# Turning the updated inverse in each doubling of a delta rule, in place of a matrix product

## The chip, the cores and the metric

The kernel runs on one core of a Trainium2 chip. The metric is the device time of one execution in microseconds (us). TensorE (PE) does matrix products and transposes into the eight banks of PSUM; VectorE (DVE) and ScalarE (ACT) work on SBUF and empty the banks; SyncE (SP) and GpSimd (POOL) issue transfers. Every engine works through its own instructions in a fixed order and waits on semaphores.

## The reference

Two layers in a row on 512 tokens of width 1024, in float32: a first block (spatial gating, differential attention, a mixture of 32 experts), then a second with a gated delta rule and stick-breaking attention. The change lies in the delta rule: four heads of width 128, in chunks of 64 tokens. For each chunk and head it needs the solution of a unit lower triangular system, then walks over the chunks:

```python
m = jnp.where(strict, beta[..., :, None] * kk * decay, 0.0)
sol = lax.linalg.triangular_solve(eye + m, rhs, left_side=True, lower=True, unit_diagonal=True)
...
def step(state, inp):
    v_new = u_c - jnp.einsum('bhck,bhkv->bhcv', w_c, state)
    o = (jnp.einsum('bhck,bhkv->bhcv', qd_c, state) + jnp.einsum('bhij,bhjv->bhiv', qk_c, v_new))
    state = state * ge_c[..., None, None] + jnp.einsum('bhck,bhcv->bhkv', kd_c, v_new)
```

## The kernel before

The delta rule works on four tiles of 128 tokens (two chunks each); all operations of a tile take the four heads together, as one 128x512 piece. The inverse of `eye + m` is built by doubling. The tensor `TT` holds the transposed inverse of the diagonal blocks of the present size, and `TI` the inverse, which is the same matrix turned. Level 0 sets blocks of two (`TT` = identity minus the masked matrix, line 1941), and `TI` is got by turning `TT` (line 1053, copied out of PSUM by ScalarE, line 2617). Each level l from 1 to 5 (`LEVELS` is 6) then takes the off-diagonal part `BT` of that level (VectorE masks it, lines 1944 and 1952), forms `Q` = BT^T TI on TensorE (line 1058), which ScalarE copies to SBUF (line 2623), and then Q^T TT (line 1062), which VectorE subtracts from `TT` (line 1965). Levels 1 to 4 form TT^T Q right behind it (line 1064), which VectorE subtracts from `TI` (line 1963), ahead of the subtraction from `TT`. Level 5 needs no new `TI`. After the levels come the products `nw` and `u` (lines 1068 and 1070), and then, tile after tile and for both chunks c of a tile, the state: `wS` (line 1076), VectorE's `vn` (line 1979), the products `kv` and `qS` (lines 1080 to 1094, whose instructions have lines 1084, 1091 and 1092), and VectorE's update of the state `S` (lines 1985 and 1988), from which the next `wS` starts. Beside the state steps of tiles 0 and 1, tiles 2 and 3 are prepared: `turn_keys`, `decays` and `turn_weighted` on TensorE, `weigh`, `weigh_turned` and `differences` on VectorE.

The order is written by generators that every engine runs in the same way. `delta_tile` yields between its pieces; it has 17 pieces: 0 (`kk`, `qk`, `qdT`), 1 (the first `TI`), 2 to 11 (two for each level), 12 (`nw` and `u`), 13 to 16 (the state). `chain(0)` runs tiles 0 and 2, `chain(1)` tiles 1 and 3; a chain waits at "state" until the tile before it is finished. A round takes one piece of each chain, and after each of the two one step of a third generator, `beside_steps`: on TensorE a step is three f32r matmuls of 128x512 (lines 543 to 545) of the projection `qb` (32 steps), then 2 * PAUSE = 10 empty steps, then `kb` (32 steps), then 10 empty ones. On VectorE and ScalarE the steps of `beside_steps` hold the splits of the next weights into two parts (ScalarE's `whi`, VectorE's `wlo`), the squares and copies of finished blocks, and after each projection its norm: sums, an inverse root, and one 128x2048 product (line 2022), which all fall into steps 33 and 34 for `qb` and 75 and 76 for `kb`; another split falls into step 38. When the chains have ended, the steps left run on without a pause.

PSUM banks are handed out by the class `Banks`: `take` gives the bank that was filled longest ago, and the first matmul into it waits until what it held before has been copied out; a projection block holds its bank until its last matmul. After the chains, TensorE turns `qb` (16 transposes, line 1225) and starts the projection `vb` (lines 1226 to 1232 and 1235 to 1238), whose four blocks are tied by hand to banks 4 to 7, and whose first step waits for what bank 4 held before:

```python
turn_block("qb", 0, beside_nat["qb"], ve["qb", 0, "normed"])
for c in range(HB):
    bank.take(("vb", 0, c), BANKS - HB + c)
value_columns(0, 0)
value_columns(0, 1)
value_columns(0, 2)
turn_block("kb", 0, beside_nat["kb"], ve["kb", 0, "normed"])
value_columns(0, 3)
claim(0, 2)
stick_scores(0)
```

Beside this ScalarE squares the whole output of the delta rule (line 2700), copies the turned `qb` (2701), makes a split, takes the root `dout` (2703) and copies the turned `kb` (2704). VectorE makes its split, builds small constants, sums the squares (line 2059), scales the output (2065, four instructions) and clears two banks (2109), for which the first scores (line 1180) of the stick-breaking attention wait.

Of the kernel before, what the change touches and what calls it, by code (L numbers as in the profile page):

```python
# [109 lines left out]
def build(nc, x, norm1_g, w_in, v_norm_g, w_s, b_s, q_norm_g, k_norm_g, lambda_q1, lambda_k1,  # L110
# [418 lines left out]
    def tensor(e):  # L529
# [509 lines left out]
        def delta_tile(i):  # L1039
            kT_, kbT, _, qdT, _, dec, MT, TI, TT, qkT, nwT, GR = sets[i % 2]  # L1040
            qT_, kd = qT_of[i], kd_of[i]
            BT, Q = kT_, kbT
            Kn, Qn, Vn = (heads(NAT[:, i, n * NH:(n + 1) * NH]) for n in (1, 0, 2))
            on.wait_ge(*ac["out", "kT", i])
            on.wait_ge(*ac["out", "kbT", i])
            mm4(i, "kk", kT_, kbT)
            on.wait_ge(*ac["out", "qT", i])
            mm4(i, "qk", kT_, qT_)
            on.wait_ge(*ve["qd", i])
            turn4(i, "qdT", Qn)  # L1050
            yield
            on.wait_ge(*ve["TT", i, 0])
            turn4(i, "TI", TT)
            yield
            for l in range(1, LEVELS):
                on.wait_ge(*ve["BT", i, l])
                on.wait_ge(*(ac["out", "TI", i] if l == 1 else ve["out", ("TI", l - 1), i]))
                mm4(i, ("Q", l), BT, TI)
                yield
                on.wait_ge(*ac["out", ("Q", l), i])  # L1060
                on.wait_ge(*ve["TT", i, l - 1])
                mm4(i, ("TT", l), Q, TT)
                if l < LEVELS - 1:
                    mm4(i, ("TI", l), TT, Q)
                yield
            on.wait_ge(*ve["rk", i])
            on.wait_ge(*ve["TT", i, LEVELS - 1])
            mm4(i, "nw", Kn, TT)
            on.wait_ge(*ve["bv", i])
            mm4(i, "u", TT, Vn)  # L1070
            yield "state"
            for c in range(2):
                R = slice(64 * c, 64 * c + 64)
                on.wait_ge(*ac["out", "nw", i])
                on.wait_ge(*(ve["state", i, c - 1] if c else ve["state", i - 1, 1] if i else ve["state0"]))
                mm4(i, ("wS", c), nwT, S)
                if i < 2:
                    (turn_weighted if c else turn_keys)(i + 2)
                yield
                ps = heads(fresh(("kv", c), i))  # L1080
                on.wait_ge(*ve["kd", i])
                on.wait_ge(*ve["out", ("wS", c), i])
                for h in range(DH):
                    m = e.matmul(ps[:, h, :], kd[R, h, :], vn[R, h, :], start=True, stop=True)
                m.then_inc(*pe.mark(("kv", c), i))
                bank.filled((("kv", c), i))
                ps = heads(fresh(("qS", c), i))
                on.wait_ge(*ac["out", "qdT", i])
                on.wait_ge(*ve["qkT", i])
                for h in range(DH):  # L1090
                    e.matmul(ps[:, h, :], qdT[:, h, :], S[:, h, :], start=True, stop=False)
                    m = e.matmul(ps[:, h, :], qkT[R, h, :], vn[R, h, :], start=False, stop=True)
                m.then_inc(*pe.mark(("qS", c), i))
                bank.filled((("qS", c), i))
                if i < 2 and c == 0:
                    decays(i + 2)
                yield
# [178 lines left out]
    def vector(e):  # L1276
# [5 lines left out]
        def settle():  # L1282

            on.wait_ge(*ve.now())
# [645 lines left out]
        def delta_tile(i):  # L1930
            kT_, kbT, _, qdT, _, dec, MT, TI, TT, qkT, nwT, GR = sets[i % 2]
            BT, Q, u_, kd = kT_, kbT, qT_of[i], kd_of[i]
            Kn, Qn, Vn = (heads(NAT[:, i, n * NH:(n + 1) * NH]) for n in (1, 0, 2))
            on.wait_ge(*pe["kk", i])
            on.wait_ge(*ac["decay", i])
            tt(MT, heads(inside("kk", i)), dec, MUL).then_inc(*ve.mark("out", "kk", i))
            on.wait_ge(*pe["qk", i])
            settle()
            tt(BT, MT, each(level[0]), MUL).then_inc(*ve.mark())
            settle()  # L1940
            tt(TT, each(ident), BT, SUB).then_inc(*ve.mark("TT", i, 0))
            yield
            settle()
            tt(BT, MT, each(level[1]), MUL).then_inc(*ve.mark("BT", i, 1))
            tt(qkT, heads(inside("qk", i)), dec, MUL).then_inc(*ve.mark("out", "qk", i))
            settle()
            tt(qkT, qkT, each(causal), MUL).then_inc(*ve.mark("qkT", i))
            yield
            for l in range(1, LEVELS):
                if l < LEVELS - 1:  # L1950
                    on.wait_ge(*pe[("Q", l), i])
                    tt(BT, MT, each(level[l + 1]), MUL).then_inc(*ve.mark("BT", i, l + 1))
                if l == 2:
                    on.wait_ge(*pe["kbT", i])
                    tt(Kn, Kn, spread(egc, i), MUL).then_inc(*ve.mark("rk", i))
                if l == 3:
                    tt(Vn, Vn, spread(betaf, i), MUL).then_inc(*ve.mark("bv", i))
                yield
                on.wait_ge(*pe[("TT", l), i])
                if l < LEVELS - 1:  # L1960
                    on.wait_ge(*pe[("TI", l), i])
                    settle()
                    tt(TI, TI, heads(inside(("TI", l), i)), SUB).then_inc(*ve.mark("out", ("TI", l), i))
                settle()
                tt(TT, TT, heads(inside(("TT", l), i)), SUB).then_inc(*ve.mark("TT", i, l))
                ve.also("out", ("TT", l), i)
                yield
            on.wait_ge(*pe["u", i])
            e.tensor_copy(u_, heads(inside("u", i))).then_inc(*ve.mark("out", "u", i))
            yield "state"  # L1970
            for c in range(2):
                R = slice(64 * c, 64 * c + 64)
                on.wait_ge(*pe[("wS", c), i])
                if c:
                    on.wait_ge(*pe[("qS", 0), i])
                elif i:
                    on.wait_ge(*pe[("qS", 1), i - 1])
                settle()
                tt(vn[R], u_[R], heads(inside(("wS", c), i))[R], ADD).then_inc(*ve.mark("out", ("wS", c), i))
                if i < 2:  # L1980
                    (differences if c else weigh)(i + 2)
                yield
                on.wait_ge(*pe[("qS", c), i])
                settle()
                tt(S, S, spread(gend[:, c * N16:(c + 1) * N16], i), MUL).then_inc(*ve.mark())
                settle()
                on.wait_ge(*pe[("kv", c), i])
                tt(S, S, heads(inside(("kv", c), i)), ADD).then_inc(*ve.mark("state", i, c))
                ve.also("out", ("kv", c), i)
                if i < 2 and c == 0:  # L1990
                    weigh_turned(i + 2)
                yield
# [176 lines left out]
    def scalar(e):  # L2169
# [440 lines left out]
        def delta_tile(i):  # L2610
            kT_, kbT, _, qdT, _, dec, MT, TI, TT, qkT, nwT, GR = sets[i % 2]
            Q = kbT
            Vn = heads(NAT[:, i, 2 * NH:3 * NH])
            on.wait_ge(*(ve["tiles clear"] if i < 2 else ve["finished", i - 2]))
            turn4(i, "qdT", qdT)
            yield
            turn4(i, "TI", TI)
            yield
            for l in range(1, LEVELS):
                on.wait_ge(*pe[("Q", l), i])  # L2620
                if l > 1:
                    on.wait_ge(*pe[("TI", l - 1), i])
                act(Q, heads(inside(("Q", l), i)), ACT.Copy).then_inc(*ac.mark("out", ("Q", l), i))
                yield
                yield
            on.wait_ge(*pe["nw", i])
            act(nwT, heads(inside("nw", i)), ACT.Copy, scale=-1.0).then_inc(*ac.mark("out", "nw", i))
            yield "state"
            for c in range(2):
                R = slice(64 * c, 64 * c + 64)  # L2630
                if i < 2 and c:
                    turn_weighted(i + 2)
                    weighted(i + 2)
                elif i < 2:
                    turn_keys(i + 2)
                yield
                on.wait_ge(*pe[("qS", c), i])
                act(Vn[R], heads(inside(("qS", c), i))[R], ACT.Copy).then_inc(*ac.mark("out", ("qS", c), i))
                yield
# [386 lines left out]
```

## Time and profile before

| | us |
|---|---|
| median of 3 runs | 1445.6 (1444.33 to 1446.9) |
| the profiled execution, its own time | 1444.63 |
| its span, first to last instruction | 1442.9 |
| TensorE busy | 1324.2 (92%) |
| VectorE busy | 660.4 (46%) |
| ScalarE busy | 495.6 (34%) |
| delta rule with what runs beside it | about 989 to 1160 of the span |

A start time in the rows counts from the first instruction of the span. Busy TensorE is not TensorE at its peak, since matmuls overlap; the pitch from one start to the next says what a matmul costs in a stream. A float32 product of 128x128 shows as two matmul records, so a product for four heads is "x8"; a turn of four heads is "x4". "PS" is PSUM. Line 1019 is any product of four heads, line 540 any transpose, line 2188 any ScalarE operation, line 1295 VectorE's part of a split.

### The profile page before, as it was taken

The numbers are of one execution on the slowest core, as the hardware profiler recorded it, in microseconds if no ns is written. First come the engines' busy times: TensorE is split into PE (matmuls) and PEld (weight loads), VectorE is DVE, ScalarE is ACT, GpSimd is POOL, SyncE is SP. The second block draws the span as 40 slices with busy tenths as digits, with TensorE's granted clock in tenths as the row PEclk, the third lists the DMA queues.
The fourth block names the chain that finished last, engine by engine and source line by source line (L and its number), as shares of the span: only waits on it lengthen the run. The fifth ranks groups of instructions, "written<-read, shape, count | busy, mean of one in ns | idle before, by whom it ended". The sixth has DMA issues, their size and how long they took to land.

```text
span 1442.9 us, 16794 instructions
## 1 busy us (share of the span) xinstructions
PE 1324.2 (92%) x7035; PEld 1018.0 (71%) x7035; DVE 660.4 (46%) x1091; ACT 495.6 (34%) x770; POOL 59.3 (4%) x70
## 2 busy tenths in 40 slices
PE   6999999999999996788887889989989988899998
PEld 5888887678766885545554468777968875488887
DVE  4454334655466446211111178657566455413253
ACT  4334234556355423011111155354232145422231
POOL 0000000000000000111111100000000001000000
PEclk9999999999999997699999999999999999899999
DMA  6222322112222368899999952102010020112331
GB/s 223 88 86 88 117 67 80 59 59 88 88 88 88 121 244 325 342 402 401 409 401 409 371 193 88 59 1 88 2 57 1 30 88 6 54 59 89 116 117 59
DMA packets 67558, 207.41 MB, mean 144 GB/s; under 512 B 9003, under 2 KB 10141, under 8 KB 55190
## 3 DMA queue, kind: packets, MB, share of 16 engines
q1 hardware_dynamic: 61234, 192.11, 35.5%
q0 software_dynamic: 5536, 12.04, 2.8%
q10 hardware_dynamic: 708, 2.13, 0.4%
q8 instruction: 57, 0.93, 0.3%
q14 instruction: 23, 0.19, 0.0%
HBM read 196.33 MB, written 17.83 MB: 148 GB/s over the span
## 4 chain that ended last, share of the span: by engine, by line
PE 71%; DVE 9%; DMA 8%; ACT 6%; issue 3%; SPq 1%; POOL 1%; ACTq 0%; POOLq 0%; DVEq 0%
PE PS L543 17%; PE PS L545 16%; PE PS L544 16%; PE PS L1019 5%; DMA work<-xn_scratch,slot_tokens 4%; PE PS L540 4%; PE PS L862 3%; DMA raw<-in_w 2%; DVE wlo L1295 2%; PE PS L890 2%; ACT work L2188 1%; SPq L2888 1%; ACT whi L2188 1%; ACT scratch L2188 1%; PE PS L707 1%
## 5 line engine op out<-in xcount | busy, mean ns | idle before, releaser
L1295 DVE TENSOR_TENSOR wlo<-raw,whi 128x2048 fp32r<-128x2048 f32 x72 | 164.9, 2291 | 277.6 <-ACT whi L2188 277.5
L2188 ACT ACTIVATE whi<-raw 128x2048 fp32r<-128x2048 f32 x72 | 137.6, 1911 | 235.3 <-PE PS L545 218.6
L543 PE MATMUL PS<-whi,hthi 128*128 128x512 f32 x480 | 195.6, 407 | 6.2 <-ACT y_plain L2188 4.1
L543 PE MATMUL PS<-hthi,whi 128*128 128x512 f32 x480 | 196.7, 410 | 0.9 <-DVE htlo L1328 0.9
L545 PE MATMUL PS<-whi,htlo 128*128 128x512 f32 x480 | 188.2, 392 | 0.0
L545 PE MATMUL PS<-hthi,wlo 128*128 128x512 f32 x480 | 187.7, 391 | 0.0
L544 PE MATMUL PS<-wlo,hthi 128*128 128x512 f32 x480 | 187.6, 391 | 0.0
L544 PE MATMUL PS<-htlo,whi 128*128 128x512 f32 x480 | 187.4, 390 | 0.0
L2188 ACT ACTIVATE work<-PS 128x512 f32<-128x512 f32 (+3 forms) x148 | 81.4, 562 | 301.0 <-PE PS L862 71.7
L543 PEld LDWEIGHTS PS<-hthi,whi 128*128 128x128 f32 x480 | 90.5, 188 | 32.5 <-issue 14.2
L543 PEld LDWEIGHTS PS<-whi,hthi 128*128 128x128 f32 x480 | 90.8, 189 | 24.5 <-ACT y_plain L2188 4.3
L545 PEld LDWEIGHTS PS<-whi,htlo 128*128 128x128 f32 x480 | 90.4, 188 | 19.4
L545 PEld LDWEIGHTS PS<-hthi,wlo 128*128 128x128 f32 x480 | 90.2, 188 | 19.4
L544 PEld LDWEIGHTS PS<-wlo,hthi 128*128 128x128 f32 x480 | 90.9, 189 | 16.0 <-issue 0.2
L544 PEld LDWEIGHTS PS<-htlo,whi 128*128 128x128 f32 x480 | 90.5, 189 | 15.7 <-issue 0.2
L540 PEld LDWEIGHTS PS<-consts,work 128*128 128x128 f32 x456 | 59.8, 171 | 48.3 <-DMA work<-xn_scratch,slot_tokens 23.7
L540 PE MATMUL PS<-consts,work 128*128 128x128 f32 x456 | 70.8, 301 | 24.8 <-DMA work<-xn_scratch,slot_tokens 15.6
L2188 ACT ACTIVATE scratch<-PS 128x512 f32<-128x512 f32 (+3 forms) x80 | 41.8, 533 | 107.8 <-PE PS L540 53.1
L543 PE MATMUL PS<-yhi,whi 128*128 128x512 f32 x192 | 75.7, 394 | 0.3 <-DVE wlo L1295 0.3
L545 PE MATMUL PS<-yhi,wlo 128*128 128x512 f32 x192 | 74.8, 389 | 0.0
L544 PE MATMUL PS<-ylo,whi 128*128 128x512 f32 x192 | 74.8, 389 | 0.0
L862 PE MATMUL PS<-y_plain,work 128*64 128x256 f32 x208 | 40.5, 417 | 4.8 <-ACT work L2188 2.5
(356 smaller groups left out, 1839.2 us busy)
## 6 DMA issues: line engine op xcount, KB each, us to landing
raw<-in_w_in SPq DMA_DIRECT2D x44, 1024.0 KB, 5.0
y_plain<-in_w SPq DMA_DIRECT2D x21, 1024.0 KB, 26.1
w_plain<-in_w SPq DMA_DIRECT2D x20, 1024.0 KB, 22.7
h_plain<-in_w SPq DMA_DIRECT2D x20, 1024.0 KB, 25.7
raw<-in_w SPq DMA_DIRECT2D x15, 1024.0 KB, 20.6
merged<-in_w SPq DMA_DIRECT2D x10, 1024.0 KB, 28.0
scratch<-in_w SPq DMA_DIRECT2D x10, 1024.0 KB, 30.1
raw<-in_w_gate SPq DMA_DIRECT2D x8, 1024.0 KB, 5.1
```

What stands on the lines that cost most here:

```text
L540: return e.transpose(o, i, ident[0:n, 0:n])
L543: e.matmul(o, lh, rh, start=start, stop=False)
L544: e.matmul(o, lh, rl, start=False, stop=False)
L545: return e.matmul(o, ll, rh, start=False, stop=stop)
L707: e.matmul(ps[:, 0:w], qT[64 * c:64 * c + 64, h, i * P:i * P + P], kT[64 * c:64 * c + 64, h, 0:w], start=True, stop=True).then_inc(*pe.mar ...
L862: t = e.matmul(ps[rows_, 0:DE], TOK[:, u, k, rows_], w[x][:, k, :], start=k == 0, stop=k == KD - 1)
L890: t = e.matmul(ps[rows_, :], HT[:, u, k, rows_], w[x][:, k, cols], start=k == 0, stop=k == 1)
L1019: m = e.matmul(ps[:, h, :], l[:, h, :], r[:, h, :], start=True, stop=True)
L1295: tt(lo, raw_place(j), as_f32(hi), SUB).then_inc(*ve.mark("lo", j))
L2188: return e.activation(o, i, f, bias=bias, scale=scale)
L2888: e.dma_start(place(raw_place(j)), src).then_inc(*raw_got[raw_slot[j]].mark(j))
```

## The change

The transposed inverse `TT` is updated first, in every level as before, and levels 1 to 4 then turn the new `TT` on TensorE and let ScalarE copy the result over `TI`. The product TT^T Q and VectorE's subtraction from `TI` are gone. A level l of 1 to 4 now has three pieces in place of two, and a tile 21 in place of 17. `beside_steps` is as it was.

```diff
@@ tensor, delta_tile
             for l in range(1, LEVELS):
                 on.wait_ge(*ve["BT", i, l])
-                on.wait_ge(*(ac["out", "TI", i] if l == 1 else ve["out", ("TI", l - 1), i]))
+                on.wait_ge(*(ac["out", "TI", i] if l == 1 else ac["out", ("TI", l - 1), i]))
                 mm4(i, ("Q", l), BT, TI)
                 yield
                 on.wait_ge(*ac["out", ("Q", l), i])
                 on.wait_ge(*ve["TT", i, l - 1])
                 mm4(i, ("TT", l), Q, TT)
+                yield
                 if l < LEVELS - 1:
-                    mm4(i, ("TI", l), TT, Q)
-                yield
+                    on.wait_ge(*ve["TT", i, l])
+                    turn4(i, ("TI", l), TT)
+                    yield
@@ vector, delta_tile
                 yield
                 on.wait_ge(*pe[("TT", l), i])
-                if l < LEVELS - 1:
-                    on.wait_ge(*pe[("TI", l), i])
-                    settle()
-                    tt(TI, TI, heads(inside(("TI", l), i)), SUB).then_inc(*ve.mark("out", ("TI", l), i))
                 settle()
                 tt(TT, TT, heads(inside(("TT", l), i)), SUB).then_inc(*ve.mark("TT", i, l))
                 ve.also("out", ("TT", l), i)
                 yield
+                if l < LEVELS - 1:
+                    yield
@@ scalar, delta_tile
                 if l > 1:
-                    on.wait_ge(*pe[("TI", l - 1), i])
+                    on.wait_ge(*pe[("TT", l - 1), i])
                 act(Q, heads(inside(("Q", l), i)), ACT.Copy).then_inc(*ac.mark("out", ("Q", l), i))
                 yield
                 yield
+                if l < LEVELS - 1:
+                    turn4(i, ("TI", l), TI)
+                    yield
```

## Rows read from the trace of the kernel before

**Rows 1.** Stretches of the span: busy us of each engine, granted clock, DMA.

```profile
1020.00:1040.00 20.00, 20.00 (x147) 18.61 (x146) 9.46 (x14) 4.95 (x8) 0.00 (x0) 1.00 0.00 1
...
1060.00:1080.00 20.00, 14.46 (x94) 12.53 (x93) 16.31 (x24) 5.89 (x10) 0.00 (x0) 0.91 0.13 40
```

**Rows 2.** The chain that ended last, one level of tiles 0 and 1.

```profile
1001.79 1.78 PE PS L1019 x16
...
1006.75 0.89 PE PS L1019 x8
1008.34 0.89 PE PS L1019 x8
1009.92 1.78 PE PS L1019 x16
```

**Rows 3.** The same chain: decays, a turn of four heads, and a state step.

```profile
1050.08 1.05 PE PS L1031 x2
...
1095.25 0.44 PE PS L540 x4
...
1145.91 0.69 DVE scratch L1979
1146.65 1.16 PE PS L1084 x8
...
1151.17 0.70 DVE scratch L1985
1151.90 0.70 DVE scratch L1988
1152.64 1.17 PE PS L1019 x8
```

**Rows 4.** VectorE and ScalarE in time: split, subtractions and a copy in level 1.

```profile
1001.98 2.29 DVE L1295 TENSOR_TENSOR wlo<-raw,whi 128x2048 fp32r<-128x2048 f32 x1 [1.45 <-ACT whi L2188]
...
1005.00 0.69 DVE L1963 TENSOR_TENSOR y_plain<-y_plain,PS 128x512 f32<-128x512 f32 x1
...
1007.68 0.60 ACT L2188 ACTIVATE y_plain<-PS 128x512 f32<-128x512 f32 x1 [5.25 <-PE PS L1019]
```

**Rows 5.** VectorE and TensorE in time: norm of `qb` and TensorE's wait.

```profile
1061.02 0.68 DVE L1287 TENSOR_REDUCE smalls<-y_plain 128x8 f32<-128x512 f32 x1
...
1063.14 2.29 DVE L2022 TENSOR_TENSOR raw<-raw,smalls 128x2048 f32<-128x2048 f32 x1
...
1067.61 1.11 PE L540 MATMUL PS<-consts,y_plain 128*128 128x128 f32 x4 [5.54 <-DVE y_plain L1941]
```

**Rows 6.** TensorE in time, from the last state step to the first scores.

```profile
1159.01 0.50 PE L543 MATMUL PS<-whi,hthi 128*128 128x512 f32 x1
...
1165.78 0.50 PE L543 MATMUL PS<-whi,hthi 128*128 128x512 f32 x1 [4.08 <-ACT y_plain L2188]
...
1180.24 0.93 PE L1180 MATMUL PS<-y_plain 64*128 64x128 f32 x8
```

**Rows 7.** ScalarE and VectorE in time behind the chains.

```profile
1162.09 1.91 ACT L2188 ACTIVATE scratch<-work 128x2048 f32<-128x2048 f32 x1
...
1174.92 2.50 DVE L2065 TENSOR_TENSOR work<-work,smalls 128x512 f32<-128x512 f32 x4
1177.80 0.70 DVE L2109 MEMSET PS<- 128x768 f32 x1 [0.38 <-ACT y_plain L2188]
```

**Rows 8.** TensorE in time: the instruction behind a wait, at two places.

```profile
632.37 1.16 PE L540 MATMUL PS<-consts,work 128*128 128x128 f32 x8 [2.69 <-DMA work<-xn_scratch,slot_tokens]
...
733.47 1.16 PE L540 MATMUL PS<-consts,work 128*128 128x128 f32 x8 [2.35 <-DMA work<-xn_scratch,slot_tokens]
```

**Rows 9.** Stretches, TensorE alone: busy us, granted clock, DMA share, GB/s.

```profile
634.00:637.00 3.00, 2.64 (x14) 0.50 1.02 382
...
733.00:736.00 3.00, 1.70 (x14) 1.00 1.02 429
...
1167.00:1169.00 2.00, 2.00 (x7) 0.50 0.00 0
```

## Prediction

> **What bounds the kernel now.** I read the stretches of the span first. In the doubling levels of tiles 0 and 1 TensorE is busy for all of 20 us while VectorE works for 9.5 and ScalarE for 5; in the 20 us around the state of those tiles TensorE stands still for 5.5 [rows 1]. DMA is nearly idle in both, so SP's queue decides nothing here, and POOL has no work. The chain that ended last says the same of the levels: products of line 1019 with the projection's f32r steps between them, and no other engine [rows 2]. So in the levels TensorE's work is the time; in the state steps, and where no projection step stands between two pieces, the hops to VectorE and back are. The change touches both, so I go through the stage round by round.
>
> **Prices.** A four-head product costs 0.89 us and, with the projection step behind it, 1.59, so the step costs 0.70 [rows 2]. A turn of four heads costs 0.44 [rows 3]. `kv` with `qS` runs from 1146.65 to just before VectorE's 1151.17, 4.4 us; `decays` 1.05 [rows 3]. VectorE's 128x512 operation takes 0.69 and about 0.1 passes before it starts, ScalarE's copy 0.60, a split 2.29 on VectorE [rows 4]. From the end of `qS` through the two updates of `S` to the next `wS` pass 1.55 us; from the end of a `wS` through `vn` to `kv` about 0.9 [rows 3].
>
> **The edits one by one.** Sixteen products TT^T Q go and sixteen turns come (four levels, four tiles): 16 x (0.89 - 0.44) = 7.2 us less on TensorE. VectorE loses sixteen subtractions, 16 x 0.69 = 11 us, ScalarE gains sixteen copies, 16 x 0.60 = 9.6. Neither moves the time of the levels by itself: it is busy half or a quarter of it [rows 1]. The new dependence is longer: product, subtraction, turn, copy, next product. With a projection step behind each piece the turn stands 0.70 + 0.89 + 0.70 = 2.3 us behind its product and needs 0.1 + 0.69; the next `Q` stands 0.70 + 0.44 + 0.70 = 1.8 behind the turn and needs 0.1 + 0.60. Covered. Without those steps the cover is gone, and here lies the cost: the sixteen extra pieces are extra rounds, and the 64 projection steps are handed out two to a round. No DMA or queue is moved.
>
> Before, tile 0 has 17 pieces, tile 2 starts in round 17, tile 1 takes up its state in round 18, tile 3 starts in round 22, and all ends in round 38; steps 1 to 32 fill rounds 0 to 15, 43 to 74 fill 21 to 38, so the last one sits behind the last state step, at 1159.01 [rows 6]. After, with 21 pieces, tile 2 starts in round 21, tile 3 in 26, and the last state step is in round 46. The projection steps stay in rounds 0 to 15 and 21 to 36. Rounds 16 to 20 are now the state of tile 0, and rounds 37 to 46 have none at all.
>
> *Rounds 2 to 15.* A pair of levels costs 2 x 1.59 + 2 x 1.59 + 2 x 1.14 = 8.62 us and carries six projection steps; before it costs 8.13, from 1001.79 to 1009.92 [rows 2], with four. One stall comes: in level 1 the split ends at 1004.27 on VectorE and the mask of tile 1 follows, so the first subtraction from `TT` can only run at 1005.00, where that from `TI` ran [rows 4]. TensorE reaches the turn at 1004.97 and goes on at 1005.8: 0.8 us. Level 1's first product started at 998.6, so level 5 ends at 998.6 + 4 x 8.62 + 6.34 + 0.8 = 1040.25.
>
> *Rounds 16 to 20, bare.* From 1040.25: four products of `nw` and `u` (3.6), `wS` and two turns (to 5.3). VectorE has two copies of `u`, a sum, the inverse root and the 2.29 us product of the norm, whose last sum to its start takes 1.44 behind the 0.68 [rows 5]; it is free at 7.3, `vn` ends at 8.0: TensorE waits 2.8. `kv`, `qS` and `decays` to 13.7; a wait of 0.6 for `S`; `wS` and the turned keys to 15.7. VectorE's order is now `S`, two weighings, the split of step 38, then `vn`, which ends at 18.7: a wait of 3.0. Tile 2's first piece follows, and its first turn starts at 27.1, at 1067.35. Before, the same norm stood ahead of tile 2's first operations, and this turn started at 1067.61 after a wait of 5.54 [rows 5]. So half of the levels' saving is already gone: I am 0.3 us and two projection steps (1.4 us) ahead, for 3.6 us of work saved.
>
> *Rounds 21 to 36.* Every piece is covered. Adding the pieces of rounds 22 to 36 (tile 1's state 13.0, tile 2 to level 5, tile 3 to level 3, 30 projection steps) gives 54.5 us, with some 0.3 of refilling: 1122.1.
>
> *Rounds 37 to 46, bare.* Here `nw` and `u` of tile 2 with the norm of `kb` on VectorE, whose 2.29 us stand ahead of `vn`; then tile 2's state against tile 3's level 4 and 5; then tile 3's `nw`, `u` and state alone. Work 29.8 us; waits 1.1 (ScalarE's copy of `Q` behind the root), 2.2 (`vn` behind the norm), 1.15 (`S`), 1.45 (`TT` behind `S`), 0.85, 1.6 and 0.85 in the last state steps, sum 9.2. The last `qS` ends at 1122.1 + 39.0 = 1161.1, against 1159.0 before [rows 6]: **2.1 us later**.
>
> *Behind the chains* comes something back. Before, TensorE turned `qb` and then waited 4.08 us until 1165.78 for a ScalarE copy [rows 6]: written out, bank 4 held the third turned `qb` block, and ScalarE came to these copies late, behind the norm of `kb` and the 1.9 us square [rows 7]. Writing out the takes of the new order, the turned blocks land in banks 0, 6, 3, 1 and bank 4 holds the last `qS`, copied out 0.7 us after its end. So `vb` starts at once. ScalarE's square starts at 1.55 behind the last `qS` and not at 3.08, since the norm of `kb` is long done, and all that hangs on it moves by 1.5. VectorE's scaling of the output started at 15.9 behind that end, took 2.5 [rows 7], and will start at 14.4; the clearing of two banks ends at 17.65. TensorE has 14.4 us of work until then. The first scores start at 17.7 instead of 1180.24 - 1159.0 = 21.2 [rows 6]: **3.5 us sooner**, with a new wait of 3.2 us. Behind them everything keeps its distances.
>
> Sum so far: 2.1 - 3.5 = -1.4 us.
>
> **The clock.** Behind a wait of 2.69 us the granted clock fell to 0.50, that is 1.2 GHz, and behind one of 2.35 it stayed at 1.00 [rows 8, 9]; it was 0.50 behind the wait of 4.08 as well [rows 9]. Such a fall costs about 1.6 us: the stretch after 1165.78 that ran at half speed lasted some 3.4 us. The old prices above contain two falls, at both long waits. The new order has three waits of about 3 us (2.8, 3.0, 3.2), all above 2.69, but my sums for them are good to 0.5 only. None falling gives -1.4, each adds 1.6, three give +3.4. I take two: +1.8.
>
> A turn's price is also where a page speaks against the change. The trace has 0.44 us for four transposes of 128x128 in float32, 0.11 each [rows 3]. The Trainium skill (TensorE: Matmul & The Clock Gate, Part 4: PE-mode transpose) gives about 275 ns for a 128x128 transpose in one kernel's context. Taken as a pitch, that would be an estimate of 16 x 4 x 0.275 = 17.6 us for the new turns against the 14.2 of the removed products: TensorE would have 3.4 us more to do and not 7.2 less, and the sum would be 10.6 us higher, near 1458. The trace differs from it and decides, so this gets no chance of its own; a page's 275 ns may be the length of one transpose that the next overlaps.
>
> **Rivals.** (1) *Slower:* all three waits let the clock fall, or the norm's and the split's place in front of `vn` costs more than 2.8 and 3.0. It decides from waits above 2.69 us on; price +3.4, 1449.0. For it: all three sums lie above that. Against: each hangs on a chain of eight terms. Part of this family is that `vb` still waits for ScalarE; then the sum is 2.1 - 1.5 + 1.6 x 2, also near +3.4. (2) *Faster:* TensorE's work bounds the stage throughout and the 7.2 us stay, 1438.4. For it: 20 of 20 us busy [rows 1]. Against: 5.5 us of waiting in the state steps, and ten more rounds without cover. (3) *Faster by a little more than can be seen:* no fall of the clock and waits shorter than mine, -3 or so, 1442.5. (4) That the change does not do what it says: both ways give the same `TI`, and the counts of instructions follow from the code; no chance worth a number.
>
> **The numbers.** The profiled execution took 1444.63 with a span of 1442.9, 1 us under the median of 1445.6; the difference of +1.8 is put on the median: 1447.4. A measurement of this kernel tells about 0.2% (2.9 us) from no change. Chances: forecast with zero to two falls 0.55, rival (1) 0.31, rivals (2) and (3) 0.14. Range: to -3.4 below, for rival (3), and to +4.9 above, for rival (1) with one wait mis-sized by 1.5: 1442.2 to 1450.5; rival (2) is left out. Faster 0.14, same 0.55, slower 0.31.
>
> **What would show it.** TT^T Q gone, and turns (x4) in its place; 21 pieces per tile; TensorE busy without a break in the levels of tiles 0 and 1 but for 0.8 us in the first; waits near 3 us ahead of both `kv` of tile 0, the first on the norm, the second on the split; no projection step behind about 1122; waits of 0.9 to 2.2 until about 1161; `vb` right behind the turned `qb`; the first scores waiting on VectorE's clearing. I am wrong if waits of more than 1 us show between 1070 and 1120, if the last `qS` ends before 1158 or after 1166, or if `vb` waits again.

## The result, and the profile after

| | before | after |
|---|---|---|
| median of the runs, us | 1446.13 (4 runs) | 1458.05 (4 runs) |
| ratio, 95% interval | | 1.0087 (1.0074 to 1.0100) |
| profiled execution: time, span | 1444.63, 1442.9 | 1455.09, 1453.3 |
| first product of the stage to the first scores | 989.39 to 1180.24, 190.9 | 989.26 to 1193.04, 203.8 |

The change makes the kernel 12 us (0.87%) slower. The forecast was 1447.4, in a range from 1442.2 to 1450.5; the measured time lies 7.5 us above that range. The profiled execution after is the fastest of its four runs, 3 us under the median. In it the stage from the first `kk` to the first scores is 12.9 us longer; some 2.4 us come back behind the stage, up to the end of the span, most of it because one stretch at the lower clock lasted 3.4 us there and 6.8 before. Every ratio here and below is taken against runs of the kernel before from the same session (medians 1446.13, then 1445.75 for e1 to e4 and 1444.76 for e5 to e7), with one slow run of the kernel before (1537.51) and one of e2_spread (3683.58) left out.

The instructions changed as the code says. The page of the changed kernel, its first part:

```profile
span 1453.3 us, 16660 instructions
PE 1331.7 (92%) x6971; PEld 1022.7 (70%) x6971; DVE 649.6 (45%) x1075; ACT 505.2 (35%) x786; POOL 59.3 (4%) x70
```

TensorE has 64 matmul records less than before: 128 of the products (eight for each of sixteen) went, 64 transposes came. VectorE has 16 operations and 10.8 us less, ScalarE 16 and 9.6 us more. But TensorE's busy time rose by 7.5 us (1324.2 before), where 7.2 less were due.

Stretches of the changed kernel's span; they answer to [rows 1], and the column before the last two is the granted clock:

```profile
1020.00:1040.00 20.00, 20.00 (x137) 18.01 (x136) 8.82 (x11) 7.69 (x11) 0.00 (x0) 1.00 0.16 53
1040.00:1060.00 20.00, 16.36 (x86) 13.11 (x85) 10.99 (x17) 7.17 (x11) 0.00 (x0) 0.75 0.00 1
1060.00:1080.00 20.00, 18.66 (x102) 15.40 (x100) 10.95 (x16) 4.70 (x8) 0.00 (x0) 0.82 0.17 53
1120.00:1140.00 20.00, 17.04 (x108) 14.96 (x106) 10.23 (x16) 5.38 (x12) 0.00 (x0) 0.89 0.17 54
1140.00:1160.00 20.00, 17.56 (x92) 14.46 (x92) 5.51 (x8) 2.98 (x5) 0.00 (x0) 0.77 0.00 1
1160.00:1180.00 20.00, 17.71 (x72) 13.95 (x71) 3.45 (x5) 4.52 (x6) 0.00 (x0) 0.66 0.00 1
```

The clock column can be read as a price: 20 us at a mean of 0.75 have lost 20 x 0.25 = 5.0 us of full speed. The five stretches below 1.00 give 5.0 + 3.6 + 2.2 + 4.6 + 6.8 = 22.2 us. Before, two stretches of this stage stood below 1.00, both at 0.91: 3.6 us. This price is an upper bound, since part of the slow time passes in waits and, as shown below, not all work takes twice as long at half the clock. The rounds that carry projection steps ran at 1.00 in both kernels. All runs agree with this: the mean clock of the whole execution was 0.955 to 0.959 in the four runs after, and 0.965 to 0.972 in the runs of the kernel before.

The waits of TensorE in time, at which the bare rounds can be followed (the bracket at the end of a line is the wait ahead of it, and what ended it):

```profile
1005.48 0.66 PE L540 MATMUL PS<-consts,y_plain 128*128 128x128 f32 x4 [0.76 <-DVE y_plain L1963]
1049.09 1.17 PE L1086 MATMUL PS<-scratch,y_plain 64*128 64x128 f32 x8 [3.63 <-DVE scratch L1979]
1061.88 1.16 PE L1086 MATMUL PS<-scratch,y_plain 64*128 64x128 f32 x8 [1.34 <-DVE scratch L1979]
1132.00 1.16 PE L1019 MATMUL PS<-scratch 128*128 128x128 f32 x8 [0.81 <-ACT scratch L2188]
1135.31 1.98 PE L1086 MATMUL PS<-scratch,y_plain 64*128 64x128 f32 x8 [2.14 <-DVE scratch L1979]
1144.58 2.08 PE L1019 MATMUL PS<-scratch,y_plain 128*128 128x128 f32 x8 [0.46 <-DVE scratch L1988]
1155.44 1.16 PE L1019 MATMUL PS<-scratch,work 128*128 128x128 f32 x8 [1.21 <-DVE scratch L1963]
1159.22 1.16 PE L1086 MATMUL PS<-scratch 64*128 64x128 f32 x8 [0.77 <-DVE scratch L1979]
1165.21 1.25 PE L1019 MATMUL PS<-scratch,work 128*128 128x128 f32 x8 [1.51 <-DVE scratch L1988]
1167.24 2.07 PE L1086 MATMUL PS<-scratch 64*128 64x128 f32 x8 [0.78 <-DVE scratch L1979]
1193.04 0.93 PE L1182 MATMUL PS<-y_plain 64*128 64x128 f32 x8 [1.07 <-DVE PS L2109]
```

These are the waits of the forecast, each where it was put and on the engine that was named, but for one of 0.6 for `S`, which did not come: together 14.5 us, against 19.6 forecast. There is none in front of `vb`: the bank walk was right as well (the 4.08 us of [rows 6] are gone).

TensorE alone in stretches of 2 us, around the waits of 3.63, 1.34, 2.14 and 1.51 (busy us, granted clock, DMA):

```profile
1046.00:1048.00 2.00, 0.00 (x0) 1.00 0.00 0
1048.00:1050.00 2.00, 0.91 (x8) 1.00 0.00 0
1050.00:1052.00 2.00, 2.00 (x8) 0.53 0.00 0
...
1060.00:1062.00 2.00, 0.66 (x4) 0.91 0.00 0
1062.00:1064.00 2.00, 2.00 (x13) 0.94 0.90 233
1064.00:1066.00 2.00, 2.00 (x7) 0.50 0.75 291
...
1068.00:1070.00 2.00, 2.00 (x9) 0.50 0.00 0
1070.00:1072.00 2.00, 2.00 (x16) 0.85 0.00 0
...
1134.00:1136.00 2.00, 0.69 (x3) 0.86 0.00 0
1136.00:1138.00 2.00, 2.00 (x10) 0.50 0.01 4
...
1148.00:1150.00 2.00, 2.00 (x12) 0.73 0.00 0
...
1164.00:1166.00 2.00, 0.79 (x7) 1.00 0.00 0
1166.00:1168.00 2.00, 1.22 (x7) 0.54 0.00 0
...
1178.00:1180.00 2.00, 2.00 (x8) 0.55 0.00 0
```

Here is what the forecast lacked. Behind the wait of 3.63 the clock was 0.50 for 10.2 us, with work on TensorE all the time, and behind a wait of only 1.34 it fell again, for 6.8 us. Towards the end of the stage it was 0.50 from about 1135.4 to 1149.1 behind the wait of 2.14, and from 1166.2 to 1179.8 behind the wait of 1.51, 13.7 us each (the wait of 0.78 came when the clock was already down). TensorE's timeline shows the cost on the pieces:

```profile
1050.19 0.80 PE L1093 MATMUL PS<-scratch,y_plain 128*128 128x128 f32 x2
1050.91 0.79 PE L1094 MATMUL PS<-scratch,y_plain 64*128 64x128 f32 x2
...
1160.30 0.49 PE L1093 MATMUL PS<-scratch 128*128 128x128 f32 x2
1160.72 0.48 PE L1094 MATMUL PS<-scratch,work 64*128 64x128 f32 x2
```

At 1.00 a pair of records of `qS` has a pitch of 0.42, at 0.50 of 0.72: half the clock makes this work 1.7 times as long, and not twice.

### The profile page after: what moved, and what is told of

It reads as the page before. It is cut to its first block, busy times and chain, and to the rows that moved or that the text cites. A ratio compares the mean times of both kernels' runs of the same rounds, so it can differ in the third digit from the quotient of the medians.

```text
span 1453.3 us, 16660 instructions
## 1 busy us (share of the span) xinstructions
PE 1331.7 (92%) x6971; PEld 1022.7 (70%) x6971; DVE 649.6 (45%) x1075; ACT 505.2 (35%) x786; POOL 59.3 (4%) x70
## 4 chain that ended last, share of the span: by engine, by line
PE 70%; DVE 10%; DMA 9%; ACT 5%; issue 3%; SPq 2%; POOL 1%; POOLq 0%; ACTq 0%; DVEq 0%
PE PS L543 17%; PE PS L545 16%; PE PS L544 16%; DMA work<-xn_scratch,slot_tokens 5%; PE PS L540 4%; PE PS L1019 4%; PE PS L862 3%; DMA w_plain<-in_w 2%; DVE wlo L1297 2%; SPq L2891 2%; ACT work L2188 1%; PE PS L1094 1%; PE PS L1093 1%; ACT whi L2188 1%; PE PS L707 1%
## 5 line engine op out<-in xcount | busy, mean ns | idle before, releaser
L543 PEld LDWEIGHTS PS<-hthi,whi 128*128 128x128 f32 x480 | 90.8, 189 | 32.5 <-issue 14.5
L545 PEld LDWEIGHTS PS<-hthi,wlo 128*128 128x128 f32 x480 | 90.4, 188 | 19.6
L2188 ACT ACTIVATE scratch<-PS 128x512 f32<-128x512 f32 (+3 forms) x88 | 46.7, 539 | 96.7 <-PE PS L540 60.6
```

Source lines behind the costliest of these rows:

```text
L543: e.matmul(o, lh, rh, start=start, stop=False)
L545: return e.matmul(o, ll, rh, start=False, stop=stop)
L2188: return e.activation(o, i, f, bias=bias, scale=scale)
```

## Experiments

Theory A: the loss is the slow clock in rounds in which TensorE has no projection step, whatever the two edited operations are. Theory B: the turn, its copy and the longer chain of dependences cost it. Theory C: the waits alone cost it.

**e1_rounds**, the rounds of the change without the change: products kept, an empty third piece (the same two lines on all three engines).

```diff
                     mm4(i, ("TI", l), TT, Q)
                 yield
+                if l < LEVELS - 1:
+                    yield
```

> The kernel before with an empty third piece in levels 1 to 4: the rounds of the changed kernel, but the products TT^T Q kept and nothing turned. Theory A (the loss is TensorE's slow clock in rounds without a projection step; turns and products play no part): the clock falls in the same places as after the change (granted clock near 0.5 for stretches of 5 to 13 us), and the time is that of the changed kernel plus the 7.2 us of work that the turns save, about 1465. Theory B (the loss comes from the turn, its copy and the longer chain of dependences): about the time before, 1446, at most 1450.

Measured: 1464.23, ratio 1.0128 (1.0101 to 1.0155). This is theory A's number (1465), 6 us above the changed kernel; a kernel with no turn of `TI` beyond level 0 loses more than the changed one. Its stretches below 1.00, TensorE alone:

```profile
1040.00:1060.00 20.00, 16.37 (x91) 0.82 0.10 40
1060.00:1080.00 20.00, 18.73 (x99) 0.76 0.16 53
...
1140.00:1160.00 20.00, 17.05 (x72) 0.71 0.00 0
1160.00:1180.00 20.00, 16.54 (x68) 0.59 0.00 1
1180.00:1200.00 20.00, 20.00 (x89) 0.77 0.21 71
```

That is 3.6 + 4.8 + 5.8 + 8.2 + 4.6 = 27 us of full speed, in the same rounds and just behind them. The extra pieces alone bring the loss, so theory B is out as its cause.

**e2_spread**, the change with the projection steps held back in eight rounds (the same lines on all three engines):

```diff
+    BARE = (4, 7, 10, 13, 28, 31, 34, 37)
...
+        round_ = 0
         while chains:
             for c in list(chains):
                 if next(c, "end") == "end":
                     chains.remove(c)
-                next(beside, None)
+                if round_ not in BARE:
+                    next(beside, None)
+            round_ += 1
```

> The changed kernel, but rounds 4, 7, 10, 13, 28, 31, 34 and 37 hand out no projection step on any engine, so that the 64 steps reach to the last state step as before the change. Each of the eight rounds then waits some 0.3 us for the copy of the turned TI. Theory A: the clock falls only where it fell before; 7.2 us of work saved less about 3 of waits: about 1442, faster than before. Theory B: the turns and copies are all still there, so about 1458.

Measured: 1441.81, ratio 0.9979 (0.9969 to 0.9989): faster than before, as theory A said (1442). The same turns, copies and dependences as in the changed kernel, 16 us less. In the stage its clock stood below 1.00 only at the two long waits that the kernel before has too, 0.83 in both stretches where that had 0.91. In the profiled execution this takes most of the stage's gain back: 190.2 us from the first `kk` to the first scores, 0.7 less than before; the other 2.3 of the 3.0 us by which its span is shorter lie outside the stage. The waits for the copy were fewer than forecast, and the two longest were 0.79 and not 0.3:

```profile
1015.58 1.16 PE L1020 MATMUL PS<-y_plain,work 128*128 128x128 f32 x8 [0.79 <-ACT y_plain L2195]
1023.86 1.16 PE L1020 MATMUL PS<-y_plain,work 128*128 128x128 f32 x8 [0.79 <-ACT y_plain L2195]
```

**e3_joined**, the turn in one piece with the next `Q`, a projection step between (TensorE's part, as it reads against the kernel before):

```diff
             for l in range(1, LEVELS):
+                if l > 1:
+                    on.wait_ge(*ve["TT", i, l - 1])
+                    turn4(i, ("TI", l - 1), TT)
+                    next(beside, None)
                 on.wait_ge(*ve["BT", i, l])
                 ...
                 mm4(i, ("Q", l), BT, TI)
-                yield
+                yield "taken" if l > 1 else None
                 ...
                 mm4(i, ("TT", l), Q, TT)
-                if l < LEVELS - 1:
-                    mm4(i, ("TI", l), TT, Q)
                 yield
```

(ScalarE's copy of the turned `TI` stands ahead of its wait for `Q`, and the main loop leaves out its own projection step after "taken".)

> The turn of TI stands in the same piece as the next Q, with one projection step between the two on TensorE, so a tile keeps 17 pieces and all projection steps stay in their old rounds. A pair of levels costs 7.24 us and not 8.13. Theory A: 7.2 us less than before less a few short waits for copies (about 0.1 each): 1439 to 1441. Theory B: the chain of dependences is the same as after the change, so it loses again: 1450 or more.

Measured: 1449.95, ratio 1.0028 (1.0018 to 1.0038). A miss: 10 us above what I had put under theory A. Its trace says why:

```profile
1088.24 1.16 PE L1019 MATMUL PS<-y_plain,work 128*128 128x128 f32 x8 [1.78 <-ACT y_plain L2188]
1120.51 1.16 PE L1019 MATMUL PS<-y_plain,work 128*128 128x128 f32 x8 [1.02 <-ACT y_plain L2188]
```
```profile
1088.00:1090.00 2.00, 1.76 (x14) 1.00 0.00 0
1090.00:1092.00 2.00, 2.00 (x10) 0.59 0.00 0
...
1100.00:1102.00 2.00, 2.00 (x15) 0.85 0.00 0
```

One projection step (0.70) does not cover the hop turn, copy, `Q`: two `Q` start 0.53 late, and two wait 1.78 and 1.02 for ScalarE. Behind the 1.78, in front of tile 1's state products, the clock fell to half for 10.2 us, another 5 us of full speed. This is not a round without projection steps; one stood right in front of the wait and the next behind the state products, at 1096.21. So theory A named the right cost, but a covered round is not safe from it. That a wait this short can stand in front of a fall is the same thing that the forecast missed, and I missed it twice.

**e4_filled**, the changed kernel with twelve useless products in the waits of the bare rounds (those without projection steps):

```diff
+        FILL = {("kv", 0, 0): 3, ("kv", 1, 0): 1, ("kv", 0, 2): 2, ("kv", 0, 3): 1, ("kv", 1, 3): 1,
+                ("wS", 1, 0): 1, ("wS", 1, 2): 1, ("wS", 1, 3): 1, ("nw", 0, 3): 1}
+
+        def filler(ps, *key):
+            for _ in range(FILL.get(key, 0)):
+                e.matmul(ps, ident, C[:, 4 * P:8 * P], start=True, stop=True)
...
```

(`filler` is called right behind `fresh`, ahead of the waits of each `nw`, `wS` and `kv`; the first number of a key is the chunk, the second the tile.)

> The changed kernel with twelve float32 products of 128x512 over constants (1.05 us each at full clock, their result is written over) put into the waits in front of kv, wS and nw of the rounds without a projection step. The work that counts is unchanged and nothing is sooner for VectorE or ScalarE. Theory A: the clock stays at 1.00 in these rounds or falls for less, and the time drops by 8 to 15 us below the changed kernel, to 1443 to 1450. If the waits themselves were the loss (theory C: my waits were undersized), the filler changes nothing or adds a few us: 1458 to 1463.

Measured: 1448.53, ratio to before 1.0022 (1.0011 to 1.0033): some 9.5 us below the changed kernel, with 12 products more. TensorE alone:

```profile
1040.00:1060.00 20.00, 17.22 (x101) 0.99 0.05 6
1060.00:1080.00 20.00, 20.00 (x100) 0.75 0.13 48
...
1140.00:1160.00 20.00, 19.20 (x112) 1.00 0.00 0
1160.00:1180.00 20.00, 19.41 (x105) 1.00 0.20 67
```

The clock stays up in the last state steps. It falls for 10.2 us behind a wait of 1.73 (5.0 us of full speed), and once more, for 3.4 us, at the end of a wait of 3.37 in front of the first scores. The filler makes nothing else start sooner, so what it gains comes through the clock: theory C is out as well, and at least these 9.5 us of the changed kernel's time are the clock's.

**e5_products_spread**: e1_rounds with the rounds of e2_spread left empty (both diffs above). It prices the swap alone.

> The products TT^T Q kept, 21 pieces a tile, the eight empty rounds of e2_spread: e2_spread without its turns. Theory A (only the slow clock in rounds without a projection step lost time, and a turn is worth 7.2 us over a product on TensorE): the order is nearly that before the change, so 1446, some 4 us above e2_spread, which gave back part of the 7.2 in waits for copies and a longer slow stretch. Theory B (turn and copy cost as much as they save): no more than 1442, the time of e2_spread.

Measured: 1446.19, ratio 1.0007 (0.9999 to 1.0016). As theory A said. Against it e2_spread is 4.4 us lower by medians from two sessions, 4.0 by their ratios: that is what turns are worth in these rounds. A little over half of the 7.2 us of TensorE's work became time. Waits for copies of 1.8 us in e2_spread's trace (0.79, 0.79 and 0.25) are part of the rest, which was not traced in full.

**e6_even**: the changed kernel, single steps held back in place of whole rounds, so that every hop has one projection step.

```diff
+    BARE = [(r, 0) for r in (4, 7, 10, 13)] + [(r, 1) for r in (5, 8, 11, 14)] + [(r, 0) for r in range(28, 36)]
...
-            for c in list(chains):
+            for n, c in enumerate(list(chains)):
...
-                next(beside, None)
+                if (round_, n) not in BARE:
+                    next(beside, None)
```

> The changed kernel with sixteen single projection steps left out of its rounds, in place of eight whole rounds, so that one step stands between any two pieces that depend on each other (the last step again falls behind the last state step). Theory A: the waits of 0.79 us for copies in e2_spread go, and a fall of the clock stays only at the two long waits that the kernel before has: 1439 to 1441, below e2_spread's 1441.8. If the time saved does not depend on where the steps stand: 1442 as e2_spread.

Measured: 1439.7, ratio 0.9966 (0.9954 to 0.9978): 5 us faster than before, the best of all. The waits for copies are gone from the levels, as expected. In its trace the wait in front of `vb` is short as well, and the clock stays up there, which I had not expected:

```profile
1160.00:1180.00 20.00, 16.33 (x87) 1.00 0.45 157
1163.16 0.50 PE L544 MATMUL PS<-whi,hthi 128*128 128x512 f32 x1 [0.75 <-ACT y_plain L2195]
1176.30 0.93 PE L1186 MATMUL PS<-y_plain 64*128 64x128 f32 x8 [2.92 <-DVE PS L2116]
```

Its stage took 1176.30 - 991.64 = 184.7 us (the start is that of its first `kk`), 6.2 less than before. The wait in front of `vb` is 3.3 us shorter than before and the one in front of the scores 2.9 longer, and no fall of the clock follows there, so part of these 6.2 us may come from there and not from the levels; this was not separated.

**e7_before_filled**: the kernel before, with four such products in its wait of 5.54 us.

```diff
+            ps = fresh("TI", i)
+            for _ in range(4 if i == 2 else 0):
+                e.matmul(ps, ident, C[:, 4 * P:8 * P], start=True, stop=True)
             on.wait_ge(*ve["TT", i, 0])
-            turn4(i, "TI", TT)
+            for h in range(DH):
+                m = turn(heads(ps)[:, h, :], TT[:, h, :])
...
```

> The kernel before with four float32 products of 128x512 over constants (4.2 us, written over by the turn) in the wait of 5.54 us in front of the first turn of tile 2; nothing else. Theory A: the clock no longer falls there; that stretch at half clock lasted 2.8 us and more in other runs, so 1.4 to 3 us less than before: 1443 to 1444.5. If the fall's price is hidden by VectorE's work behind it: no difference.

Measured: 1445.11, ratio 1.0002 (0.9993 to 1.0011): no difference, where 1.4 to 3 us were expected. The clock did stay at 1.00 in the stretch from 1060 to 1080, and in the profiled execution the way from the first `kk` to the first product of `vb` is 1.5 us shorter than before: 174.9 us (992.10 to 1166.98) for 176.4 (989.39 to 1165.78). But the wait of 4.08 in front of `vb` is still there, and behind it the lower clock now lasted 6.8 us and not 3.4:

```profile
1166.98 0.80 PE L543 MATMUL PS<-whi,hthi 128*128 128x512 f32 x1 [4.08 <-ACT y_plain L2194]
1160.00:1180.00 20.00, 15.93 (x76) 0.83 0.30 106
```

Up to the first scores 0.7 us of the gain is left. All runs together say the same: the mean clock of the whole execution is 0.969 in the eleven runs of this kernel and 0.969 in the 23 of the kernel before. So the filler removed a fall that cost about what I had priced it at, in its place, and won no clock on the whole. Why the next one lasted longer is not shown.

## Why the prediction was wrong, point by point

- **Work taken off TensorE**: right. Turns for products are worth 7.2 us of its work; by medians, e2_spread against e5 shows 4 us of it as time where the projection steps are spread, and e6_even against the kernel before 5 us. That the measured 1458 is also the sum which the prediction worked out for transposes of 275 ns is luck: four turns of `TI` take 0.36 us here (0.09 each) from their start to the next instruction's at full clock, and e1_rounds, without these turns, took 6 us longer still.
- **Rounds and cover**: right. 21 pieces leave rounds 16 to 20 and 37 to 46 without projection steps, and TensorE waits there where the forecast has it. Of the single sizes the wait on the norm was larger (3.63 for 2.8), those on the split and on `S` smaller (1.34 for 3.0; 0.46 for 1.15), both behind work at half clock, with which TensorE arrives later; the one at the scores was 1.07 for 3.2, likewise.
- **Behind the chains**: right. `vb` starts without a wait, and the first scores came 18.0 us behind the last `qS` (1175.0 to 1193.04), 17.7 forecast, 21.2 before. But this last `qS` came 14 us later than forecast (1161.1), past the 1166 that the prediction had set as a sign of being wrong.
- **The step that failed is the clock**, the term "such a fall costs about 1.6 us", with "two of three" waits letting it fall: 3.2 us in all. Four falls came, and half speed lasted 10.2, 6.8, 13.7 and 13.7 us: 22.2 us of full speed in the changed kernel against 3.6 before. What of this became time can be read from TensorE's busy and idle time in the stage. It was busy for 188.6 us, before for 179.5, so 9.1 more; it stood still for 15.2, before for 11.4, so 3.8 more; together the measured 12.9. Its work fell by 7.2, so the lower clock cost 9.1 + 7.2 = 16.3 us more than before. That fits the two prices seen above: TensorE was busy for 43.1 us at half speed, before for 6.5, and with 0.42 to 0.50 us lost in each of them this is 15 to 18 us.
- **Its size** came from one fall, the one at 1165.78, which lasted 3.4 us. That was no fixed price: behind the wait of 5.5 us that the kernel before, e2_spread, e3_joined, e5 and e6_even all have in front of the same turn, half speed lasted 3.4 us in the first and 6.8 in the other four.
- **Its condition**, waits above 2.69 us, came from two waits in other stages (2.35 no, 2.69 yes). In the changed kernel the clock fell behind waits of 1.34, 1.51 and 2.14, while it stayed up behind waits of 1.91 (e3_joined, in front of `vb`), 2.11 (e7) and 2.92 (e6_even, in front of the scores). So the length of a wait alone does not decide, and the bound was too high for the bare rounds, where several waits follow each other closely.
- **Rival (1)** named the right mechanism and the right side, but with the same price for a fall, so that it ended at 1449. The profile of before does not show what half speed costs in the bare rounds, and I bounded it from one row; the bound from above should have been the whole length of the bare rounds at half speed, some 10 us and more on the slow side.

## What to carry to other kernels

Where generators on several engines hand out filler work by pieces, an edit that adds a piece moves the filler: count the rounds before counting the operations, and hold filler back in the covered rounds so that it lasts to the end. Price a round that loses its cover by its waits and, as a second term, by its whole length at half of TensorE's clock; a single fall seen elsewhere does not bound it. Judge filler that is to hold up the clock by the time of the whole kernel, since a fall removed in one place was made up for in the next (e7). A change that reads as slower can be a faster one with the filler in the wrong place: here the same edit gave +0.9% as it stood and -0.3% with sixteen steps held back.

## What the runs showed of the hardware

A stretch at the lower clock (0.50, that is 1.2 GHz) lasted 10 us and more with TensorE at work: 10.2 us without any pause in the changed kernel (1050 to 1060), and in e3_joined (1090 to 1100), and 13.7 us with one pause of 0.46 (changed kernel, 1135 to 1149). Behind these falls ran float32 products of four heads and the 64-row `kv` and `qS`. In the kernel before both falls of the stage lasted 3.4 us, one with float32 turns and products behind it (1067.61), one with f32r products of 128x512 (1165.78); in other runs the same two places had 6.8 us (the first in e2_spread, e3_joined, e5 and e6_even, the second in e2_spread and e7). So the kind of product alone does not explain the length.

The length of the wait ahead does not say whether the clock falls: it fell behind 1.34, 1.51, 1.73 (e4_filled) and 1.78 (e3_joined), and stayed at 1.00 behind 1.91 (e3_joined), 2.11 (e7) and 2.92 (e6_even). Float32 products over constants, put into waits, kept it up through the last state steps of e4_filled. What sets the fall and its length was not isolated: the kinds of products and the short waits between them always came together here.

At half speed `qS` took 1.7 times as long (0.72 for 0.42 a pair), sixteen transposes 1.9 times (3.67 us in the changed kernel at 1175.03, 1.91 before at 1159.80).
